# The even mixer's softmax division for 32 units: from VectorE to GpSimd

## The reference, cut to what matters

```python
s_loc = jnp.where(valid, q @ k.T * scale, NEG)
s_ctx = q @ k_ctx.T * scale
p = softmax(concat([s_loc, s_ctx, s_sink], -1))
o = p[..., :nloc] @ v_local + p[..., nloc:nloc + lc] @ v_ctx
```

## Time and profile before

| what | us |
|---|---|
| median of 3 executions | 3321.45 (3320.80 to 3321.55) |
| span of the profiled execution, first to last instruction | 3318.4 |
| the median less that span | 3.05 |
| busy in the span: TensorE, VectorE, ScalarE, GpSimd | 3205.3, 2250.6, 1231.3, 88.4 |

### The profile page before, as it was taken

How to read it: one execution, slowest core, us unless ns; L and a number is a source line. 1 busy time by engine, 2 the same in 40 slices (tenths; PEclk the granted TensorE clock), 3 DMA queues, 4 the chain that set the end, 5 groups by cost and what they waited for, 6 DMA issues and landing times. The chain is left out here.

```text
span 3318.4 us, 50677 instructions
## 1 busy us (share of the span) xinstructions
PE 3205.3 (97%) x20394; PEld 2946.0 (89%) x20394; DVE 2250.6 (68%) x3840; ACT 1231.3 (37%) x2091; POOL 88.4 (3%) x189
## 2 busy tenths in 40 slices
PE   8999999988999999989999999989999999999999
PEld 7999999977889999989999999878888888877777
DVE  4979896478577777777777776665333656466654
ACT  4111112256553343364433343553222432334332
POOL 0000000001100000010000000000000000000000
PEclk9999999999999999999999999999999999999999
DMA  5545553200222222232222222112322320222232
GB/s 220 185 171 184 184 174 124 75 33 27 52 82 68 88 80 88 90 86 66 69 101 83 89 80 87 52 48 91 100 94 95 130 77 27 67 75 70 70 103 95
DMA packets 95288, 313.83 MB, mean 95 GB/s; under 512 B 11424, under 2 KB 15712, under 8 KB 93520
## 3 DMA queue, kind: packets, MB, share of 16 engines
q1 hardware_dynamic: 88128, 290.04, 25.4%
q0 software_dynamic: 6928, 20.55, 2.2%
HBM read 300.06 MB, written 4.19 MB: 92 GB/s over the span
## 5 line engine op out<-in xcount | busy, mean ns | idle before, releaser
L687 PE MATMUL psum<-zh,wh 128*128 128x512 f32 (+4 forms) x2352 | 759.2, 369 | 27.6 <-DVE sx L3784 9.4
L656 ACT ACTIVATE wh<-raw 128x512 fp32r<-128x512 f32 (+3 forms) x551 | 447.1, 817 | 842.8 <-PE psum L687 446.5
L687 PE MATMUL psum<-zh,rawl 128*128 128x512 f32 (+4 forms) x2352 | 737.4, 359 | 0.0
L687 PE MATMUL psum<-zl,wh 128*128 128x512 f32 (+4 forms) x2340 | 733.8, 359 | 0.0
L666 DVE TENSOR_TENSOR rawl<-raw,wh 128x512 fp32r<-128x512 f32 (+3 forms) x551 | 502.1, 926 | 242.6 <-ACT wh L656 241.2
L687 PEld LDWEIGHTS psum<-zh,wh 128*128 128x128 f32 x2352 | 432.3, 190 | 80.0 <-issue 33.7
L1165 PE MATMUL psum<-formq,wh 128*128 128x386 f32 x1848 | 479.0, 340 | 15.2 <-DVE formq L968 4.7
L687 PEld LDWEIGHTS psum<-zh,rawl 128*128 128x128 f32 x2352 | 434.7, 190 | 41.5
L687 PEld LDWEIGHTS psum<-zl,wh 128*128 128x128 f32 x2340 | 432.4, 190 | 40.4 <-issue 3.5
L1165 PEld LDWEIGHTS psum<-formq,wh 128*128 128x128 f32 x1848 | 336.7, 189 | 21.3 <-DVE rawl L666 6.7
L771 DVE SCALAR_TENSOR_TENSOR h<-psum,mod,h 128x512 f32<-128x512 f32 (+1 forms) x288 | 169.8, 627 | 187.8 <-PE psum L687 187.5
(11 more groups left out here) (497 smaller groups left out, 4589.6 us busy)
## 6 DMA issues: line engine op xcount, KB each, us to landing
raw<-in_wup SPq DMA_DIRECT2D x176, 512.0 KB, 4.0
modw<-in_mod_w SPq DMA_DIRECT2D x128, 512.0 KB, 3.5
raw<-in_w_sw SPq DMA_DIRECT2D x36, 512.0 KB, 3.5
raw<-in_wdn SPq DMA_DIRECT2D x64, 256.0 KB, 3.7
raw<-in_wdn SPq DMA_DIRECT2D x32, 448.0 KB, 3.3
adaw<-in_ada_w SPq DMA_DIRECT2D x8, 1024.0 KB, 16.2
raw<-in_wdn SPq DMA_DIRECT2D x16, 512.0 KB, 3.9
raw<-in_od_in SPq DMA_DIRECT2D x16, 512.0 KB, 3.5
```

Source lines behind the costliest of these rows:

```text
L656: nc.scalar.activation(hi_of(n, i), x, ACT.Copy).then_inc(w_hi, 1)
L687: last = nc.tensor.matmul(psum[:, at + to:at + to + e - s], w[:, q * P:(q + 1) * P], x[:, q, s:e], start=(q == 0 and j == 0), stop=(q == s ...
```

## The change

For the first 32 units VectorE stops after the reciprocal, which now raises `at_p`. GpSimd gets the multiplication of the probabilities: in its loop, behind the query remainder of unit i, it multiplies the probabilities of unit i-3, after a wait for its own remainder and for that unit's reciprocal. Its end raises a semaphore (`ev_scaled`, one that already stood at 1 from an earlier use), and the transposes of a first-half unit wait for that in place of `at_p`. GpSimd's remainder of unit i waits, from i = 4 on, for the multiplication of unit i-4 as well. Units 32 to 47 are as before.

```diff
             for i, u in enumerate(EUNITS):
+                if 4 <= i < SECOND_S + 4:
+                    pool.wait_ge(ev_scaled, SCALED + i - 3)
                 if i < 4:
                     pool.wait_ge(eq_hi, EQ_HI)
                 else:
                     pool.wait_ge(at_pc, i - 3)
                 nc.gpsimd.tensor_tensor(u.place[u.beside], u.query, u.place[u.r], ALU.subtract).then_inc(zq_lo, 1)
+                if 3 <= i < SECOND_S + 3:
+                    divided = EUNITS[i - 3]
+                    pool.wait_ge(zq_lo, i + 1)
+                    pool.wait_ge(at_p, i - 2)
+                    nc.gpsimd.tensor_scalar(divided.probs(), divided.probs(), rinv[:, divided.k:divided.k + 1], None,
+                                            ALU.mult).then_inc(ev_scaled, 1)
...
             def transposes(i):
                 u = EUNITS[i]
-                pe.wait_ge(at_p, i + 1)
+                if i < SECOND_S:
+                    pe.wait_ge(ev_scaled, SCALED + i + 1)
+                else:
+                    pe.wait_ge(at_p, i + 1)
...
                 link(dve, "dve", nc.vector.tensor_tensor(rsum[:, r], rsum[:, r], esink[:, r], ALU.add))
-                link(dve, "dve", nc.vector.reciprocal(rinv[:, r], rsum[:, r]))
-                nc.vector.tensor_scalar(u.probs(), u.probs(), rinv[:, r], None, ALU.mult).then_inc(at_p, 1)
+                ins = nc.vector.reciprocal(rinv[:, r], rsum[:, r])
+                if i >= SECOND_S:
+                    link(dve, "dve", ins)
+                    ins = nc.vector.tensor_scalar(u.probs(), u.probs(), rinv[:, r], None, ALU.mult)
+                ins.then_inc(at_p, 1)
```

More of the change, by code:

```diff
@@ L1965, in build @@
         at_sink, zq_lo = S("att_sink"), S("ev_query_lo")
-        ek_hi, eq_hi, ek_lo = e_sq, e_sq, e_kn
+        ek_hi, eq_hi, ek_lo, ev_scaled = e_sq, e_sq, e_kn, e_perm
         EK_HI, EQ_HI, EK_LO = 6, 9, 2
@@ L1970, in build @@
         E_SUM, E_SPR, E_ROT, E_VT, E_S, E_PT, E_OUT, E_MIX = 3584, 2048, 3072, 2048, 1024, 2048, 3072, 3584
+        SCALED = 1
         KROW, VROW, QROW, VVROW, UROW = 0, 2, 3, 7, 11
```

## The result

The changed kernel takes 3330.16 us (median of 12 executions) against 3321.6 us for the kernel before on the same chip (12 executions): a ratio of 1.0023, with a 95% interval of 1.0015 to 1.003. (The ratios in this document aren't quotients of the two medians: here the medians differ by 8.6 us, the means by 7.7.) It is slower, outside the forecast range of 3318 to 3328 and on the side of the first rival. A second set of executions (8 against 24) gave 3329.58 against 3322.03 us, 1.0027, interval 1.0016 to 1.0037.

A forecast was written before the change was run, and what follows sets the result against it. TensorE bounds the kernel, busy 3205.3 of 3318.4 us; 1.0 us gained from VectorE's freed time less 0.5 lost in late transposes makes 0.5 us faster, with the median's 3.05 above the span 3321.0 us, range 3318 to 3328.

The forecast's parts named there:

- the first rival: GpSimd's multiplication runs at the remainder's pace, in the loop copy, remainder, multiplication, transposes: 15 us lost, 1.0 gained, 3335 us; chance 8%.
- what the multiplication costs: On GpSimd, 0.61, 0.76 and 0.30 us for 512, 640 and 256 columns, in proportion to a 64x512 COPY of 608 ns.
- the table of the loss: Transposes' lateness by the 512-wide multiplication's duration, same slacks: 0.5 us lost at 0.61, 2.9 at 1.0, 6.4 at 1.3, 15 at 1.85.
- The rest of the sum: Over the 32 units: 1.0 us gained from VectorE's freed time less 0.5 lost in late transposes, 0.5 us faster.
- the seven named: Units 5, 7, 15, 17, 27, 30 and 31, whose transposes come late; only 7 (0.31 us) and 30 (0.15) lose time.
- Taking VectorE's work away: VectorE loses 15.8 us busy in 32 units; only 1.0 us gained, in waits before scores.
- The 5 us between a remainder and its scores: GpSimd's remainder also waits for an earlier multiplication at no cost, since its scores come some 5 us behind it.
- The second rival: VectorE's two-input operations go first in units 5, 7, 12, 15 and 27, each multiplication 0.95 later: 3324.4 us; chance 9%.
- work that nobody waits for: Units 5, 6 and 7: multiplication starts first, VectorE's two-input operations are held 0.1 to 0.3 us, counted as nothing.
- the COPY of the earlier trace: A COPY of 2 columns took 1.03 us, ending together with VectorE's two-input L666, as evidence of contention.

## Why the prediction was wrong

**The step that failed is the term "what the multiplication costs".** I took the COPY's 0.61 us for 512 columns, with the remainder's 1.85 as the other end, since the multiplication reads one tensor as the copy does. It measured 1.61, past the 1.38 us from which the prediction's first rival decides, so 15 transposes waited and not seven. The kind of operands was the wrong thing to compare by: with two tensors in, the same product takes 1.04 us. By the table of the loss (6.4 us at 1.3, 15 at 1.85) 1.61 us gives 11 lost and 1.0 gained, 3332 us; it came to 3330. The mechanism was on record, with a chance of 8%, and the upper end of the range was cut just below it.

**The rest of the sum held where it could be tried.** With the copy's duration the seven late units were the seven named, and the time was that of before (ratio 0.9995, interval 0.9987 to 1.0004; the sum had said 0.5 us less). Taking VectorE's work away was worth little, as said. The 5 us between a remainder and its scores covered the remainder's later start, as said: no scores wait for it.

**The table of the loss was wrong twice, with opposite signs.** It allowed only for the idle time directly behind each late unit. In fact other waits shrank too: before scores by 5.8 us, in the gated branch by 2.4, while the waits for the multiplication grew by 14.2, so idle time rose 5.8 us. And it left out the clock, though the long waits at 690 and 814 us had a lower level behind them in the trace of before (0.51 and 0.60 in these stretches; the mean of the whole stretch is 0.97):

```profile
695.00:700.00 5.00, 5.00 (x65) 4.55 (x64) 3.45 (x9) 3.71 (x8) 0.22 (x1) 0.51 0.01 3
815.00:820.00 5.00, 3.29 (x22) 3.06 (x24) 4.18 (x13) 4.94 (x15) 0.90 (x2) 0.60 0.01 2
```

**The second rival** (VectorE's two-input operations first) didn't happen: in no unit was such an operation under way when the multiplication began, and in 31 of 32 units the multiplication kept its duration to 0.01 us; unit 31's, beside a two-input operation of the projection's input, took 2.08 us. VectorE was held instead, by 0.13 to 0.32 us in units 5, 7, 22 and 30. For the first two the prediction had 0.1 to 0.3 us in work that nobody waits for; with the product of two tensors the hold reached 0.78 us, and the time was still that of before.

## What to carry to other kernels

Before moving an operation to an engine on which no row shows it, take the widest of the bounds for the range, or look for a row of the same operation: the number of tensors read says little about the pace on GpSimd. Place it in the new engine's list by its own inputs; behind an operation that waits for something later, it inherits that wait. And where a stall is added in front of TensorE, look at the granted clock of the next microseconds before counting only the stall.

## What the runs showed of the hardware that was not expected

- GpSimd on 128 partitions in f32, for 512 columns: copy 613 ns, product of two tensors 1042, product with a constant 1491, product with a column of factors 1565 to 1606. The Trainium skill's "GPSIMD Engine Reference", section "Engine selection", has one-input operations at about line rate and two-input ones about half as fast as on VectorE. The copy is near that, if VectorE's 510 ns for a one-input product of this width is the measure; for the product by a scalar the measurement says otherwise, and it decides: it is slower than the product of two tensors.
- GpSimd's multiplication held VectorE's two-input operations for its first part only. L2224 started 0.22 us behind the start of unit 7's, ended before it, and took 1.27 us, where the median of its eight runs in the same profile is 0.95. The four such operations (L2224, L2228) that began 0.20 to 0.32 us behind a multiplication's start ended 1.28, 1.49 and 1.59 us behind that start for 256, 512 and 640 columns, as if they had begun 0.33, 0.54 and 0.64 us behind it; the eight that began from 0.48 us on took 0.95 to 0.97. The product of two tensors held VectorE nearly to its end. This is unit 5 in the timed profile of that kernel, where L2228 ended 0.82 us behind the product:

```profile
715.13 1.25 POOL L2018 TENSOR_TENSOR ev_s<-ev_s,rinv 128x640 f32<-128x640 f32 x1
715.47 1.73 DVE L2228 SCALAR_TENSOR_TENSOR gpart<-gpart,ev 128x768 f32<-128x768 f32 x1
```

The Trainium skill's "SBUF — State Buffer", section "Who interferes with whom", has the later of the two wait for the whole instruction of the earlier. The trace comes near that for the product of two tensors and for the COPY of the earlier trace rows, and doesn't agree for the product by a column, and the measurement decides.

- TensorE's clock: behind the 1.85 us stall of unit 5, with 1.15 us busy of 3.0, it was granted 0.52 for 3.5 us in one execution of the changed kernel and 1.00 in the other; with 2.46 us busy in that stretch it was 1.00 in the one profile taken.
